# Splitting a dependency by token group and starting A2 tasks between the last spatial groups of A1, in an eight-core hybrid decoder block

## What is computed

```python
h = _rmsnorm(x, norm_g[l])
proj = jnp.einsum('bsd,dn->bsn', h, w_in[l])
a_u, a_v, a_gate, b_qkv, b_gate, g_a, g_b = jnp.split(proj, split_pts, axis=-1)
# _gmlp_sgu: spatial gating within chunks of 128 positions
u = jax.nn.gelu(u)
v = _layernorm(jax.nn.gelu(v), ln_g, ln_b)
s = jnp.einsum('gij,bcjgh->bcigh', tril(w_s), vc) + b_s
ya = (u * s) * jax.nn.silu(a_gate)
ya = jnp.einsum('bsc,cd->bsd', ya, w_oa[l])
...
merged = jax.nn.sigmoid(g_a) * ya + jax.nn.sigmoid(g_b) * yb
x = x + jnp.einsum('bsd,de->bse', merged, w_out[l])
```

## Time and profile before

| | us |
|---|---|
| median of six runs | 1106.12 |
| lowest and highest of them | 1087.87, 1109.85 |
| all six | 1109.85, 1106.15, 1087.87, 1109.09, 1106.08, 1090.64 |
| profiled execution, its own time | 1089.76 |
| its span on the slowest core (core 1) | 1088.6 |
| spans of the eight cores | 1078.8 to 1088.6 |

### The profile page before, as it was taken

One profiled execution on the slowest core, in us unless ns is written; L12 is line 12 of the kernel. 1 busy time (PEld: TensorE's weight loads), 2 busy tenths in 40 slices (PEclk: granted clock), 3 DMA queues, 4 the chain that ended last, 5 costly groups with the idle time before them and its releaser, 6 DMA issues.

```text
span 1088.5 us, 20782 instructions; the slowest of 8 cores (1078.8 to 1088.6 us)
## 1 busy us (share of the span) xinstructions
PE 958.7 (88%) x7264; PEld 543.5 (50%) x7264; DVE 597.9 (55%) x878; ACT 545.7 (50%) x962; POOL 161.7 (15%) x161
## 2 busy tenths in 40 slices
PE   1478769997899979999798977799999899999898
PEld 1246454664656646665466733444444344444343
DVE  5556794557775677766776765456553122222233
ACT  4566867658676686766866554653332111111100
POOL 2000000010000100000010000034554333341100
PEclk9789889999899998999999989889999899999999
DMA  9943521040330403303073000024464833451197
GB/s 220 201 126 59 117 70 17 4 39 2 31 31 2 40 2 30 31 2 30 2 95 53 2 1 1 1 20 40 39 54 60 86 34 36 44 47 12 59 293 267
DMA packets 101621, 62.56 MB, mean 57 GB/s; under 512 B 88720, under 2 KB 92816, under 8 KB 101520
## 3 DMA queue, kind: packets, MB, share of 16 engines
q0 software_dynamic: 91728, 26.61, 25.2%
q1 hardware_dynamic: 7344, 25.71, 7.0%
q10 hardware_dynamic: 2448, 8.91, 2.7%
HBM read 79.44 MB, written 8.39 MB: 81 GB/s over the span
## 4 chain that ended last, share of the span: by engine, by line
PE 68%; ACT 11%; DVE 9%; issue 6%; DMA 5%; ACTq 0%; DVEq 0%; POOL 0%; SPq 0%; POOLq 0%
PE pb L290 60%; PE pb L520 3%; DMA xt_25_70<-xo 3%; PE pb L493 2%; DMA wr_9_51<-w_in 1%; ACT junk_74 L341 1%; ACT lr_21_64 L389 1%; PE pb L387 1%; PE pb L357 1%; DMA wout_11314<-w_out 1%; ACT lr_21_64 L391 1%; PE pb L762 1%; DVE sta_74_9277 L730 1%; ACT lr_22_65 L389 1%; ACT lr_20_63 L389 1%
## 5 line engine op out<-in xcount | busy, mean ns | idle before, releaser
L290 PE MATMUL pb<-hTo_46,wr_5_47 128*128 128x512 bf16 x288 | 74.2, 405 | 3.6 <-DVE hTo_46 L359 2.7
L290 PE MATMUL pb<-hTo_46,wr_10_52 128*128 128x512 bf16 x320 | 75.9, 381 | 0.0
L290 PE MATMUL pb<-hTo_46,wr_6_48 128*128 128x512 bf16 x320 | 75.4, 380 | 0.0
L290 PE MATMUL pb<-hTo_46,wr_9_51 128*128 128x512 bf16 x288 | 69.7, 387 | 4.9 <-DMA wr_9_51<-w_in 4.9
L290 PE MATMUL pb<-Wv_7899,hTo_46 128*128 128x512 bf16 x256 | 59.7, 392 | 0.0
L290 PE MATMUL pb<-wout_11314,mT_11313 128*128 128x512 bf16 x256 | 57.1, 387 | 2.8 <-POOL mT_11313 L900 2.8
L896 DVE SCALAR_TENSOR_TENSOR m_92_11319<-ta_88_11315,pb 128x512 f32<-128x512 f32 x16 | 11.0, 688 | 78.4 <-PE pb L290 73.7
L896 DVE SCALAR_TENSOR_TENSOR m_93_11320<-ta_89_11316,pb 128x512 f32<-128x512 f32 x16 | 11.0, 688 | 73.2 <-PE pb L290 73.2
L472 DVE CAST Vaug_66<-pb 128x512 bf16<-128x512 f32 (+1 forms) x72 | 47.8, 664 | 4.3 <-PE pb L290 4.2
L290 PEld LDWEIGHTS pb<-hTo_46,wr_5_47 128*128 128x128 bf16 x288 | 29.2, 103 | 39.1 <-issue 10.8
L290 PEld LDWEIGHTS pb<-hTo_46,wr_10_52 128*128 128x128 bf16 x320 | 30.5, 98 | 35.7 <-issue 1.1
(11 more groups left out here) (294 smaller groups left out, 2139.2 us busy)
## 6 DMA issues: line engine op xcount, KB each, us to landing
xf_96_13089<-xo ACTq DMA_DIRECT2D x6, 512.0 KB, 4.9
out<-ot_99_13092 SPq DMA_DIRECT2D x6, 512.0 KB, 4.7
wr_5_47<-w_in POOLq DMA_DIRECT2D x11, 256.0 KB, 5.9
wr_6_48<-w_in POOLq DMA_DIRECT2D x11, 256.0 KB, 6.5
wr_9_51<-w_in POOLq DMA_DIRECT2D x11, 256.0 KB, 5.4
wr_10_52<-w_in POOLq DMA_DIRECT2D x11, 256.0 KB, 6.5
xf_97_13090<-xo ACTq DMA_DIRECT2D x5, 512.0 KB, 4.9
xf_98_13091<-xo ACTq DMA_DIRECT2D x5, 512.0 KB, 5.2
```

The lines of the kernel that those rows point to most:

```text
L290: c.op(PE, lambda kc=kc: tn.matmul(ps, lhs_fn(kc), rhs_fn(kc), start=(kc == 0), stop=(kc == nk - 1)), reads=reads, writes=[pbuf], inc=(kc ...
```

## The change

sT's single dependency buffer becomes four, one per token group. The allocation of A2's buffers and the definition of its task move in front of A1's last loop. In the loop's last group, G == 3, the buffers are allocated and three weight pairs are loaded in front of spatial group 12, and two A2 tasks are issued after the evacuation of each of the chunks 12 to 15, eight in all, none of them of token group 3. The loop of A2 leaves those eight out.

```diff
     sT, b_sT, off = ar.alloc("sT", [128, 8, T], F32, P_BASE + 32768)
+    b_sTg = [Buf(f"sTg{g}") for g in range(4)]
+    ar.live.extend((P_BASE + 32768, P_BASE + 32768 + 65536, b_) for b_ in b_sTg)
...
                                             ps[:].rearrange("p (j i) -> p j i", j=4), AF.Copy),
-                 reads=[b_ps], writes=[b_sT])
+                 reads=[b_ps], writes=[b_sTg[tc // 4]])
...
-                 reads=[b_sT, b_cf, b_cst], writes=[b_sa])
+                 reads=[b_sTg[g], b_cf, b_cst], writes=[b_sa])
...
+    a2_early = [(0, 0), (0, 1), (0, 2), (1, 0), (1, 1), (1, 2), (2, 0), (2, 1)]
+    a2_done = set()
...
+            if tc == 12:
+                a2_alloc()
+                for j in range(3):
+                    a2_load(j)
             pss = a1_spatial(tc)
             if tc + 8 < NCH:
                 a1_s1(tc + 8)
             a1_evac(tc, pss)
             if k == 1 and G + 1 < 4:
                 a1_ln(G + 1)
+            if G == 3:
+                for _ in range(2):
+                    j, g = a2_early.pop(0)
+                    a2_task(j, g)
+                    a2_done.add((j, g))
...
         for g in range(4):
-            a2_task(j, g)
+            if (j, g) not in a2_done:
+                a2_task(j, g)
```

More of the change, by code:

```diff
@@ L773, in a1_evac, with a2_alloc @@
                                             ps[:].rearrange("p (j i) -> p j i", j=4), AF.Copy),
-                 reads=[b_ps], writes=[b_sT])
+                 reads=[b_ps], writes=[b_sTg[tc // 4]])
             banks.put((ps, b_ps))
+    A2 = {}
+    def a2_alloc():
+        A2["yaT"], A2["b_yaT"], _ = ar.alloc("yaT", [128, 8, T], BF16, P_BASE)
+        A2["gu"], off = mkpool("gu", 2, [128, 512], F32, A_TMP)
+        A2["t2"], off = mkpool("tg2", 2, [128, 512], F32, off)
+        A2["m2"], off = mkpool("m2", 2, [128, 512], F32, off)
+        A2["sa2"], off = mkpool("sa2", 2, [128, 512], F32, off)
@@ new lines, in build_program, with a2_load, a2_task, s1 @@
+    pcst = list(cst[:].ap[0])
+    a2w = {}
+    def a2_load(j):
+        if j < 8 and j not in a2w:
+            a2w[j] = (load_w(COL_U + j * 128), load_w(COL_G + j * 128))
+    def a2_task(j, g):
+        S = {}
+        tsl = slice(g * 512, (g + 1) * 512)
+        (wu, b_wu), (wg, b_wg) = a2w[j]
+        def s1():
+            pu, b_pu = S["pu"] = banks.get()
+            mm_group(pu[:], b_pu, lambda kc: wu[:, kc, :], lambda kc: hTo[:, kc, tsl], 8, [b_wu, b_hTo[g]])
+            pg, b_pg = S["pg"] = banks.get()
+            mm_group(pg[:], b_pg, lambda kc: wg[:, kc, :], lambda kc: hTo[:, kc, tsl], 8, [b_wg, b_hTo[g]])
+            gu, b_gu = S["gu"] = A2["gu"].get(); tg, b_tg = S["tg"] = A2["t2"].get()
+            c.op(ACT, lambda: sc.activation(gu[:], pu[:], AF.Gelu_apprx_tanh), reads=[b_pu], writes=[b_gu])
+            c.op(ACT, lambda: sc.activation(tg[:], pg[:], AF.Tanh, scale=0.5), reads=[b_pg], writes=[b_tg])
+            banks.put(S["pu"])
+        def s2():
+            pg, b_pg = S["pg"]; gu, b_gu = S["gu"]; tg, b_tg = S["tg"]
+            m2, b_m2 = A2["m2"].get()
+            sa, b_sa = A2["sa2"].get()
+            cstb = bass.AP(cst, j * 128, [pcst, [0, 4], [1, 128]])
+            c.op(DVE, lambda: ve.scalar_tensor_tensor(sa[:].rearrange("p (a i) -> p a i", a=4),
+                                                      sT[:, j, tsl].rearrange("p (a i) -> p a i", a=4),
+                                                      cf_t[:, F_LNG + j:F_LNG + j + 1], cstb, ALU.mult, ALU.add),
+                 reads=[b_sTg[g], b_cf, b_cst], writes=[b_sa])
+            c.op(POOL, lambda: gp.tensor_tensor(gu[:], gu[:], sa[:], ALU.mult), reads=[b_gu, b_sa], writes=[b_gu])
+            A2["sa2"].put((sa, b_sa))
+            c.op(DVE, lambda: ve.scalar_tensor_tensor(m2[:], tg[:], 1.0, pg[:], ALU.add, ALU.mult),
+                 reads=[b_tg, b_pg], writes=[b_m2])
+            c.op(DVE, lambda: ve.scalar_tensor_tensor(A2["yaT"][:, j, tsl], gu[:], 0.5, m2[:], ALU.mult, ALU.mult),
+                 reads=[b_gu, b_m2], writes=[A2["b_yaT"]])
+            banks.put(S["pg"]); A2["gu"].put(S["gu"]); A2["t2"].put(S["tg"]); A2["m2"].put((m2, b_m2))
+        pipe.submit(s1, s2, lag=1)
@@ L777, in build_program, with c1_load @@
+    c1w = {}
+    def c1_load(j):
+        if j < 8 and j not in c1w:
+            c1w[j] = (load_w(COL_GA + j * 128), load_w(COL_GB + j * 128),
+                      load_w(j * 128, src=w_oa), load_w(j * 128, src=w_ob, rows=4))
+    a2_early = [(0, 0), (0, 1), (0, 2), (1, 0), (1, 1), (1, 2), (2, 0), (2, 1)]
+    a2_done = set()
     a1_s1(0)
@@ L803, in build_program @@
                 a1_ln(G + 1)
[L805 to L839, removed]
-                 reads=[b_sT, b_cf, b_cst], writes=[b_sa])
[L841 to L856, removed]
+            if G == 3:
[3 more added lines that the diff above has]
+                    a2_done.add((j, g))
+    yaT, b_yaT = A2["yaT"], A2["b_yaT"]
     a2_load(0)
```

## The result

| | kernel before | changed kernel |
|---|---|---|
| profiled execution, us | 1089.76 | 1090.33 |
| median of the runs, us | 1106.12 (20 runs) | 1106.08 (10 runs) |
| lowest and highest, us | 1087.87, 1196.34 | 1092.82, 1217.21 |
| ratio of this comparison | | 1.0123, 95% 1.0067 to 1.0179 |

The forecast was 1089.8 us and no difference that can be measured. The two medians agree to 0.04 us, and the comparison still puts the changed kernel 1.2% above the one before, with an interval that leaves out 1. The two lists differ at their low end: four of the 20 runs before lie under 1095 us, and one of the ten after.

What follows compares the result with a forecast made beforehand. TensorE work was taken to bound the kernel, 68% of the span; split, ScalarE order and weight loads at 0 and the reordered stretch at +0.07 us on 1089.76 gave 1089.8 us, range 1084 to 1110.

Steps and rivals of the forecast that it cites:

- All three holes stay, and the early groups run behind spatial group 12: TensorE, end of A1: idle times of 1.69, 1.32 and 5.17 us remain; filling them had chance 0.05.
- The sum from group 12 to C1: TensorE, spatial group 12 to the start of C1: 114.47 us forecast against 114.40, a cost of +0.07 us.
- the half-speed term: TensorE, 713.11 to 716.7: A2 matmuls at 1.2 GHz, half of that stretch lost, 1.80 us.
- No table load between Copy and Gelu or Tanh: ScalarE, among the early tasks: mixing these functions adds no table switch; one would take 1.28 us.
- The fourth pair's lead is enough: Load of wr_11 and wr_12 in A2: three tasks of lead leave 4.8 and 4.6 us slack, cost 0.
- The rival's price for a late load: First use of wr_11: a 15.5 us load makes TensorE wait 6.2 us, costs 9.0, giving 1098.8; chance 0.08.
- The level: Whole kernel: +0.07 on the profiled execution's 1089.76 us gives 1089.8 us.
- Cost and gain are 0: Split of sT's buffer: VectorE's first read could start earlier, hidden by 111.03 us of unbroken TensorE matmuls; 0 us.
- That the comparison would show no change: Whole kernel, measured against the one before: within 2% at chance 0.92, faster 0.04, slower 0.04.
- a median of the changed kernel can come out anywhere in that spread, so the range covers it: Whole kernel: six runs of one program lie between 1087.87 and 1109.85 us; the range was 1084 to 1110.
- about what a measurement of this kernel can tell from no change: Whole kernel: 2%, about 22 us, taken as the smallest difference that can be measured.

Runs made afterwards that it cites:

- e4: Changed kernel with the same eight early tasks issued one chunk earlier, behind the evacuations of chunks 11 to 14; median 1102.25 us, ratio 1.0010.
- e5: Changed kernel with sT as one dependency buffer again, so the early tasks alone; median 1103.18 us, ratio 0.9980.
- e6: Changed kernel with the eight early tasks two chunks earlier, behind the evacuations of chunks 10 to 13; median 1084.35 us in four runs, ratio 0.9883.
- e7: Changed kernel with the load of the fourth weight pair issued two tasks later; median 1107.37 us, ratio 1.0059.
- e3: Kernel before with the split of sT's buffer alone, no early tasks; median 1107.03 us, ratio 1.0027.
- e1: Changed kernel measured again, unaltered, against the kernel before; median 1107.01 us, ratio 1.0053.
- e8: The kernel of e4 once more, unaltered, as a second sample against the kernel before; median 1091.53 us, ratio 0.9923.
- e9: Changed kernel with one dependency buffer for each of the 32 evacuations in place of one per token group; median 1102.39 us, ratio 1.0005.

## Why the prediction was right and wrong

Right, by its own steps:

- *All three holes stay, and the early groups run behind spatial group 12.* 1.69, 1.33 and 5.01 us were found. The reason given was program order, and e4 shows it: the same eight tasks one place earlier fill the hole and take 6.5 us off. In e4, e5 and e6 a hole goes only where ready groups stand in front of the waiting one. The Trainium skill (TensorE: Matmul & The Clock Gate, Step-by-step: what each phase is for) says that matmuls stay in program order; the traces agree.
- *The sum from group 12 to C1.* Forecast 114.47, measured 114.52 on core 7 (before: 114.40). Its terms: 3.41 us for the first A2 group; 0.45 for a spatial group at 2.4 GHz; the clock's rise 4.57 us behind group 12 where 4.4 was taken. With the rise at 715.28 the half-speed term is 1.88, half of 711.52 to 715.28, and the sum 0.81 + 110.51 + 1.35 + 1.88 = 114.55.
- *No table load between Copy and Gelu or Tanh.* None stands around the evacuation at 721.05. The Trainium skill (ScalarE: Activation LUTs, Table sets: the hidden batching unit) counts copy to every table set; the trace agrees.
- *The fourth pair's lead is enough.* No wait, though the slack is 3.3 and 3.6 us and not 4.8 and 4.6. The issue came 1.1 us behind the task, as taken; the landings took 6.0 and 6.5 us in place of 4.4 and 5.4. The rival's price for a late load holds in kind: in e7 a wait of 4.74 costs 7.6 us on its core. Its 15.5 us was not the slowest landing, though: the DMA view of the kernel before has 17.3 us for the load of wr_10 and 17.9 for that of wr_11 right behind it, by which the rival's sum would be about 11.5 us and not 9.0.
- *The level.* 1089.8 us was forecast for the profiled execution, 1090.33 was measured; core 1 has a span of 1088.4 us, against the 1088.6 us of core 1 in the profile before. That it fits to half a us is in part luck: 17 executions of the kernel before in which all eight cores were undisturbed lie between 1089.07 and 1094.12 us.

Wrong, in two steps:

- *"Cost and gain are 0" for the split of sT's buffer.* The step looked only at the first reader on VectorE. The split also takes away a wait on the writer's side, between evacuations on ScalarE that had named one and the same buffer, and these stand on the path to group 12: 0.2 us off the hole (5.17 to 4.98 in e3, and 5.17 again in e5). Up to the first matmul of yaT about 0.1 us of it is left (124.68 us in e3, 124.79 before), since the clock rises 4.6 us behind group 12 in e3 (core 5: a slice from 715 to 716 at 0.67, group 12 at 711.07) and rose 4.4 behind it before. The term is small beside everything else, but it is a gain where none was seen.
- *That the comparison would show no change.* The step that failed is the sentence that "a median of the changed kernel can come out anywhere in that spread, so the range covers it". It let the range carry the scatter of single runs and took for granted, with "about what a measurement of this kernel can tell from no change" for 2%, that the comparison of two groups would then show no difference. It gave that comparison no spread of its own, and the comparison came out at 1.0123 with an interval of ±0.6% that leaves out 1. What the runs showed in its place is no cost in the kernel: the stretch that the change touches takes 124.70 to 124.75 us on the eight cores against 124.77 to 124.81, the ratio fell to 1.0053 in e1, one program against itself gives 1.0054, each half of the change alone gives 1.0027 and 0.9980, and undisturbed cores differ by 0.3 us in the other direction. A cost of 1.2% would be 13 us, nearly three times what the late weight pair costs in e7, and that cost, 4.8 us, is plain in the mean spans. So the 1.2% belongs to that comparison and not to the kernel, which is concluded by exclusion: no second comparison came out as far from 1 without a change in the trace to match, and what made the first one do so stays open.

The version that beats both kernels is e4 (with e6 beside it): the early tasks from behind spatial group 11 on. It is 6.5 us (0.6%) shorter than the kernel before by the mean span of undisturbed cores, and 5.9 us shorter than the changed kernel in TensorE's timeline. Its ratios by whole runs are 1.0010 in e4 and 0.9923 (0.9858 to 0.9989) in e8, of which only the second is clear of 1.

## What to carry to other kernels

To fill a hole on an engine that runs in program order, ready work must be issued ahead of the instruction that waits: look up which instruction the idle time stands in front of, and place the first filler one instruction earlier, since one place behind it the filler here earned nothing. When a comparison gives a per cent that no stage of the trace holds, run the unaltered program against itself before looking for a mechanism, and add up the stretch that was changed on every core. Splitting a buffer can remove a wait between its writers as well as one of its reader, so follow both sides.

## What the runs showed of the hardware that was not expected

- Six evacuations on ScalarE that name one buffer take 4.04 us, with four buffers 3.83, with one each 3.04 us: the removed waits of an instruction on the one before it on its own engine are worth up to 1.0 us over six copies (e5, the changed kernel, e9).
- A shorter hole was not worth its length. In e9 TensorE reached group 12 0.80 us sooner, and the granted clock stayed at 0.50 for 5.8 us behind it in place of 4.6, which gave 0.61 back; in e3 it was 0.19 us sooner, and 0.08 went back.
- A hole of 2.06 us in front of a late load (e7, core 0) leaves the granted clock at 1.00 while TensorE stands still; it falls to 0.50 only at about 760.4, 1.3 us behind the restart, and stays there for 3.4 us of full work.
